# A two-layer transformer kernel: keys cut from 256 to 160 in its second attention, forgetting sums formed once, and the exponentials of a recurrence moved in the order of work

## The reference, cut to what matters

```
h  = x + rms(mixer(rms(x)))              # mixer: 8 heads "fox" + 8 heads "hgrn", w_in, w_out
h  = h + rms(conv_ffn(rms(h)))           # 3-tap convolution along the tokens, w_up, w_down
h  = h + rms((p @ w_proj) * sigmoid(rms(h) @ w_gate))
h  = h + neighbourhood_attention(rms(h)) # 16 heads, na_w_qkv, na_w_o
out= h + relu(rms(h) @ w1)**2 @ w2
```

## Time and profile before

| what | value |
|---|---|
| median of 3 runs | 2419.09 us |
| the profiled execution's own time | 2418.97 us |
| its span, first to last instruction | 2417.2 us |
| TensorE busy | 2405.5 us, 12352 records |
| VectorE busy | 1525.5 us |
| ScalarE busy | 1216.5 us |
| GpSimd busy | 110.4 us |
| TensorE's granted clock | 1.00 of full throughout |
| DMA | 451 MB, 57.6% of 16 engines by the weight queue |

### The profile page before, as it was taken

One profiled execution on the slowest core, in us unless ns is written; L12 is line 12 of the kernel. 1 busy time (PEld: TensorE's weight loads), 2 busy tenths in 40 slices (PEclk: granted clock), 3 DMA queues, 4 the chain that ended last, 5 costly groups with the idle time before them and its releaser, 6 DMA issues.

```text
span 2417.2 us, 30523 instructions
## 1 busy us (share of the span) xinstructions
PE 2405.5 (100%) x12352; PEld 2055.4 (85%) x12352; DVE 1525.5 (63%) x1788; ACT 1216.5 (50%) x1596; POOL 110.4 (5%) x122
## 2 busy tenths in 40 slices
PE   8999999999999999999999999999999999999999
PEld 7898988788888888888877888888888888888887
DVE  6676765577567657667666666665655555554654
ACT  6455444565445445445565655555443443443442
POOL 0221310000000000000000211000000000000000
PEclk9999999999999999999999999999999999999999
DMA  9566565556655655656655565455556556566664
GB/s 311 138 173 173 156 198 188 179 174 195 201 183 184 202 181 188 204 176 195 210 186 168 181 193 167 148 179 182 186 188 195 185 193 194 187 193 193 191 200 149
DMA packets 327132, 451.27 MB, mean 187 GB/s; under 512 B 14528, under 2 KB 209344, under 8 KB 326352
## 3 DMA queue, kind: packets, MB, share of 16 engines
q1 hardware_dynamic: 324592, 440.52, 57.6%
q0 software_dynamic: 2256, 8.80, 1.2%
q10 hardware_dynamic: 144, 0.01, 0.0%
HBM read 447.17 MB, written 2.10 MB: 186 GB/s over the span
## 4 chain that ended last, share of the span: by engine, by line
PE 97%; DVE 2%; issue 0%; ACT 0%; DMA 0%; POOL 0%; DVEq 0%; ACTq 0%
PE main L566 92%; PE aux L566 3%; DVE LO L1152 1%; DVE AR L1152 1%; PE aux L579 1%; PE aux L677 0%; PE aux L695 0%; ACT HI L810 0%; DVE AR L1329 0%; DVE XT L1155 0%; DMA COL<-in_cols 0%; DVE AR L1155 0%; PE aux L661 0%; DVE AR L1293 0%; DVE AR L1294 0%
## 5 line engine op out<-in xcount | busy, mean ns | idle before, releaser
L1152 DVE TENSOR_TENSOR LO<-RAW,HI 128x1024 fp32r<-128x1024 f32 (+2 forms) x833 | 1008.1, 1232 | 614.6 <-ACT HI L810 613.5
L810 ACT ACTIVATE HI<-RAW 128x1024 fp32r<-128x1024 f32 (+2 forms) x833 | 850.1, 1045 | 621.6 <-PE main L566 574.7
L566 PE MATMUL main<-XT,HI 128*128 128x512 f32 x2944 | 739.1, 393 | 0.0
L566 PE MATMUL main<-HI,YT 128*128 128x512 f32 x2240 | 693.6, 390 | 0.0
L566 PEld LDWEIGHTS main<-XT,HI 128*128 128x128 f32 x2944 | 529.8, 189 | 95.2
L566 PEld LDWEIGHTS main<-HI,YT 128*128 128x128 f32 x2240 | 420.5, 188 | 87.2
L566 PE MATMUL main<-HI,XT 128*128 128x512 f32 (+1 forms) x1472 | 458.1, 386 | 7.8 <-DVE LO L1152 7.7
L566 PE MATMUL main<-LO,YT 128*128 128x512 f32 x1120 | 435.8, 389 | 0.0
L566 PEld LDWEIGHTS main<-XT,LO 128*128 128x128 f32 x2944 | 401.6, 190 | 28.9
L566 PE MATMUL main<-XT,LO 128*128 128x256 f32 x2944 | 410.4, 282 | 0.0
L566 PEld LDWEIGHTS main<-HI,XT 128*128 128x128 f32 x1472 | 275.0, 188 | 60.0 <-DVE XT L1155 6.9
(11 more groups left out here) (87 smaller groups left out, 710.9 us busy)
## 6 DMA issues: line engine op xcount, KB each, us to landing
RAW<-in_mlp_w SPq DMA_DIRECT2D x256, 512.0 KB, 4.1
RAW<-in_w_up SPq DMA_DIRECT2D x176, 512.0 KB, 4.7
RAW<-in_na_w_qkv SPq DMA_DIRECT2D x96, 512.0 KB, 4.3
RAW<-in_w_in SPq DMA_DIRECT2D x95, 512.0 KB, 4.2
RAW<-in_w_down SPq DMA_DIRECT2D x88, 512.0 KB, 4.8
RAW<-in_w_out SPq DMA_DIRECT2D x32, 512.0 KB, 4.3
RAW<-in_w_ple_gate SPq DMA_DIRECT2D x32, 512.0 KB, 4.4
RAW<-in_na_w_o SPq DMA_DIRECT2D x32, 512.0 KB, 4.1
```

The source lines that it names most:

```text
L566: return L.e.matmul(out, l, r, start=start, stop=stop, skip_group_check=True)
L810: return L.e.activation(out, x, f, **kw)
L1152: return L.e.tensor_tensor(out, x, y, op)
```

## The change

1. **Token order.** From w_out's input on, the tokens lie by column of the grid and not by row (token = 4 x column + row). Where the natural order is needed or produced (fox and hgrn outputs, the FFN's input and its output, the residual's load, the final store), the reading or writing pattern is strided by 4 numbers (`by_column`, `by_row`). Neighbourhood attention itself needs no inner reordering any more.
2. **160 of 256 keys.** In that order, the keys that 128 queries need lie in one band of 160. Scores, bias, softmax and the copy after the transposes work on 2 x 160 numbers. The output product becomes three products of 160, 64 and 96 columns. The transposes keep their four, over a buffer whose borders are zeroed once.
3. **Forgetting sums once.** A step `f_sums` at slot 60 forms the sums of all 8 heads with two products, ScalarE writes them negated to CN (8 partitions), and for each head GpSimd's queue loads its row to 128 partitions (`f_row`), GpSimd adds the causal mask (`f_decay`), and VectorE adds the result to the logits in two instructions in place of one. `f_score` keeps two of its five products.
4. **Level exponentials.** The exponential leaves `h_decay` and becomes `h_exp`, one slot later, so it stands on ScalarE behind the next slot's rounding and no longer ahead of it.
5. **Second half of hgrn:** `h_out` and `h_rms` move from slots 105 and 107 to 108 and 110.

```diff
+        put(mid, j0 + 6, "h_exp", hf, 0)
         put(mid, j0 + 6, "h_weigh", hf, 0)
...
                 put(mid, at, "h_decay", hf, lvl)
+                put(mid, at + 1, "h_exp", hf, lvl)
                 put(mid, at + 1, "h_weigh", hf, lvl)
...
-        put(mid, j0 + 33, "h_out", hf)
-        put(mid, j0 + 35, "h_rms", hf)
+        put(mid, (j0 + 33, 108)[hf], "h_out", hf)
+        put(mid, (j0 + 35, 110)[hf], "h_rms", hf)
...
+    put(mid, 60, "f_sums")
-        for what, j in (("f_decay", j0 - 6), ("f_score", j0 + 2), ...
+        for what, j in (("f_row", j0 - 5), ("f_decay", j0 - 3), ("f_score", j0 + 2), ...
...
+        def by_column(ap):
+            return ap.rearrange("p (c r) -> p r c", r=4) ...
+        def by_row(ap, r=4):
+            return ap.rearrange("p (r c) -> p r c", r=r) ...
...
+            def f_sums():                                            # TensorE
+                mm(out[0:8, 0:256], LS[:, 0, :], tri, True, False)
+                mm(out[0:8, 128:256], LS[:, 1, :], tri[:, 0:128], False, True)
...
-                mm(out[:, 0:128], q[:, 0:128], k[:, 0:128], True, False)
-                mm(out[:, 0:128], B[:, 0, :], tri[:, 0:128], False, True)
-                mm(out[:, 128:384], q[:, 128:256], k, True, False)
-                mm(out[:, 128:384], B[:, 0, :], tri, False, False)
-                mm(out[:, 256:384], B[:, 1, :], tri[:, 0:128], False, True)
+                mm(out[:, 0:128], q[:, 0:128], k[:, 0:128], True, True)
+                mm(out[:, 128:384], q[:, 128:256], k, True, True)
...
-                mm(out[:, 0:256], q[:, 0:128], k, True, True)
-                mm(out[:, 256:512], q[:, 128:256], k, True, True)
+                mm(out[:, 0:160], q[:, 0:128], k[:, 96:256], True, True)
+                mm(out[:, 160:320], q[:, 128:256], k[:, 0:160], True, True)
...
-                mm(out[:, 0:256], VN[:, 0, ...], P[:, 0, :], True, False)
-                mm(out[:, 0:256], VN[:, 1, ...], P[:, 1, :], False, True)
+                mm(out[:, 96:256], v[0], P[:, 0:160], True, False)
+                mm(out[:, 96:160], v[1], P[:, 256:320], False, True)
+                mm(out[:, 0:96], v[1], P[:, 160:256], True, True)
...
+                    if ph == 1:                                      # ScalarE, FFN input; VectorE alike
+                        dst, src = by_row(dst), by_column(src)
...
+                if n < 22:                                           # ScalarE, FFN output; VectorE alike
+                    dst, src = by_column(dst), by_row(src)
...
+                out = banks[bank["f_score", h]]                      # VectorE
+                L.wait_ge(S("g_lb"), 2 * h + 2)
+                tt(P[:, 0:128], out[:, 0:128], CD[h % 2], ALU.add)
+                tt(P[:, 128:384], out[:, 128:384], CB[h % 2], ALU.add)
...
+            def f_row(h):                                            # GpSimd's queue
+                L.wait_ge(S("a_cn"), 1)
+                if h > 1:
+                    L.wait_ge(S("v_fl"), h - 1)
+                load(f"d_cb{h % 2}", CB[h % 2], <row h of CN, to 128 partitions>)
...
             def f_decay(h):                                          # GpSimd
+                L.wait_ge(S(f"d_cb{h % 2}"), 16 * (h // 2 + 1))
+                L.e.tensor_tensor(CD[h % 2], B[:, 0:128], causal, ALU.add)
+                L.e.tensor_tensor(B[:, 128:256], B[:, 128:256], causal, ALU.add)
```

More of the change, by code:

```diff
@@ L161, in stages @@
                 put(mid, at + 1, "h_far", hf)
-        put(mid, j0 + 33, "h_out", hf)
-        put(mid, j0 + 35, "h_rms", hf)
+        put(mid, (j0 + 33, 108)[hf], "h_out", hf)
+        put(mid, (j0 + 35, 110)[hf], "h_rms", hf)
         put(mid, (j0 + 35, 120)[hf], "h_gated", hf)
         put(mid, (j0 + 38, 122)[hf], "h_turn", hf)
+    put(mid, 60, "f_sums")
     for hp in range(4):
         j0 = 88 + 8 * hp
-        for what, j in (("f_decay", j0 - 6), ("f_score", j0 + 2), ("f_norm", j0 + 3), ("f_turn", j0 + 5), ("f_out", j0 + 7)):
+        for what, j in (("f_row", j0 - 5), ("f_decay", j0 - 3), ("f_score", j0 + 2), ("f_norm", j0 + 3), ("f_turn", j0 + 5), ("f_out", j0 + 7)):
             for h in (2 * hp, 2 * hp + 1):
@@ L273, in stage @@
                 take(("h_turn", rest[0], t), ("v_hyl", 2 * rest[0] + t + 1))
+        elif name == "f_sums":
+            take(("f_sums",), ("a_cn", 1))
         elif name == "f_score":
@@ L380, in program @@
         PF, PTF = [ar(16896, 384), ar(11776, 384)], [ar(17280, 384), ar(12160, 384)]
-        LB = [ar(19200, 2, 128), ar(12544, 2, 128)]
+        CB = [ar(19200, T), ar(12544, T)]
+        CD = [CST[:, C_CM + 128 + i * 128:C_CM + 256 + i * 128] for i in range(2)]
         MSKF = ar(8192, 8, 128)
@@ L527, in store @@
             def store(nb):
-                cs = slice(nb * 512, nb * 512 + 512)
-                L.wait_ge(S("v_h"), 56 + 2 * nb + 2)
-                L.e.dma_start(outv[:, :, cs], H[:, :, cs]).then_inc(S("d_out"), 16)
+                for t in range(2):
+                    L.wait_ge(S("v_h"), 56 + 2 * nb + t + 1)
+                    put(t, nb * 512, 512)
             def fetch_gate(nb):
@@ L727, in gate_value @@
                 x.then_inc(S("p_e"), 1)
-            work = {"e": gate_value, "turn": turn, "xq": turn_half, "h_score": h_score, "h_far": h_far, "h_out": h_out, "h_turn": h_turn, "f_score": f_score,
+            work = {"e": gate_value, "turn": turn, "xq": turn_half, "h_score": h_score, "h_far": h_far, "h_out": h_out, "h_turn": h_turn, "f_sums": f_sums, "f_score": f_score,
                     "f_turn": f_turn, "f_out": f_out, "n_turn": n_turn, "n_score": n_score, "n_prob": n_prob, "n_out": n_out,
@@ L1353, in h_turn @@
                     out = banks[bank["h_turn", hf, t]].rearrange("p (h t) -> p h t", h=4)
[L1354 to L1355 removed]
+                    c0 = 8 + 4 * hf
+                    hi, lo = [by_column(YT[:, c0:c0 + 4, i, :])[:, :, 2 * t:2 * t + 2, :] for i in range(2)]
+                    tt(lo, by_row(out, 2), hi.bitcast(F32), ALU.subtract).then_inc(S("v_hyl"), 1)
             def f_score(h):
@@ L1388, in n_turn @@
                 if i == 0:
-                    for r in range(2):
-                        rows = slice(r * 64, r * 64 + 64)
-                        x = L.e.tensor_scalar(dst[:, :, rows], src[:, :, rows][:, :, ::-1], gc, SCALE, ALU.mult, ALU.mult)
+                    x = L.e.tensor_scalar(dst, src[:, :, ::-1], gc, SCALE, ALU.mult, ALU.mult)
                 else:
@@ L1722, in bias0 @@
                     bias_rows(h)
-            work = {"h_abs": h_abs, "h_decay": h_decay, "h_weigh": h_weigh, "h_out": h_out, "f_decay": f_decay,
+            work = {"h_abs": h_abs, "h_decay": h_decay, "h_weigh": h_weigh, "h_out": h_out, "f_row": f_row, "f_decay": f_decay,
                     "n_prob": n_prob, "first_loads": first_loads, "more_loads": more_loads, "last_loads": last_loads,
@@ L1790, in constants @@
     c[:, C_TRI + 128:C_TRI + 256] = 1.0
-    col = 63 - i % 64
-    start = np.clip(col - 8, 0, 48)
-    k = np.arange(64)[None, :]
-    c[:, C_WIN:C_WIN + 64] = np.where((k >= start[:, None]) & (k < start[:, None] + 16), 0.0, NEG)
+    for t in range(2):
+        start = np.clip(63 - 32 * t - i // 4 - 8, 0, 48)
+        k = 24 - 24 * t + np.arange(40)[None, :]
+        c[:, C_WIN + 40 * t:C_WIN + 40 * t + 40] = np.where((k >= start[:, None]) & (k < start[:, None] + 16), 0.0, NEG)
     m = np.zeros((128, 8, 128), np.float32)
```

138 lines of the change are left out of this document (80 added, 58 removed).

## The result

The changed kernel takes 2403.23 us (median of 4 runs, 2402.82 to 2403.74), the kernel before 2419.19 us in the same session (4 runs, 2419.09 to 2419.53). The ratio is 0.9934, 95% interval 0.9917 to 0.9951: 16.0 us less. Predicted were 2403.0 us and 2400 to 2410.5. The profiled execution took 2403.74 us, its span is 2402.0; before 2418.97 and 2417.2.

A forecast was written before the change was run, and what follows sets the result against it. TensorE was taken as the bound. From 2418.97 us, 14.1 of products (7.0 + 5.2 + 2.6 - 0.7) and 2.1 of stops came off and 0.3 for strided passes was added: 2403.1, forecast 2403 us, range 2400 to 2410.5.

The forecast's parts named there:

- What bounds the kernel: Whole kernel: TensorE alone sets the time while ScalarE waits for HI; product time taken out comes off the end.
- Fox: Fox's `f_score`, five products to two: 3.07 us for two heads falls to 1.31, saving 7.0 us for eight heads.
- Scores: Neighbourhood scores, 256 to 160 columns: 3.45 us for four heads falls to 2.16, saving 5.2 us for four groups.
- Outputs: Neighbourhood output, two products to three: 1.73 us for two heads falls to 1.40, saving 2.6 us for sixteen.
- The sums: `f_sums` at slot 60: two added products and a switch to an aside and back add 0.7 us (0.5 to 0.9).
- Exponentials: hgrn's 344-column stage: exponentials behind the rounding remove 2.1 us of TensorE stops; hgrn's second half has none to give back.
- The second rival: Fox's slots: VectorE becomes the bound, 60 of 70 us, and fox's 7.0 us are lost: 2410 us; chance 0.07.
- Strided passes: ScalarE and VectorE passes with a step of 4 numbers: 0.3 us added at the FFN's input; cover at its output.
- The first rival: FFN's input: strided passes cost more than plain ones where TensorE waits for them, +3.7, 2407 us; chance 0.12.
- The third rival: FFN's output: strided passes, from factor 4, outrun 4.0 us of cover; at factor 6, 2460 us; chance 0.03.
- The cover of the DMA and of GpSimd: Fox's forgetting rows: loads come seven slots (20 us) earlier, GpSimd has 48 of 75 us free; nothing booked.
- the unnamed losses: Anywhere in the kernel: losses not named in the prediction that eat most of the gain; chance 0.05.

The follow-up runs named there:

- run 3: Only the forgetting sums formed once and loaded, on the kernel before, with exponentials and `h_out` at their old slots: 2416.38 us, ratio 0.9988.
- run 1: The changed kernel with each level exponential put back at the slot of its decay, ahead of the next rounding: 2407.99 us, ratio 0.9953.
- run 7: The changed kernel with ScalarE's strided pass at the FFN's output made four times instead of once: 2463.82 us, ratio 1.0185.
- run 9: The changed kernel with ScalarE's strided pass at the FFN's output made twice instead of once: 2408.06 us, ratio 0.9954.
- run 6: The changed kernel with the FFN's output written in natural order, without strided writes, leaving out the reordering of tokens: 2403.28 us, ratio 0.9934.
- run 10: The changed kernel with GpSimd's `f_decay` right behind the load of its row, so GpSimd waits for the DMA: 2403.81 us, ratio 0.9935.
- run 11: The changed kernel with final stores going to 128 consecutive rows, leaving out the order of the output's rows: 2402.78 us, ratio 0.9932.
- run 2: The kernel before with nothing but the level exponentials moved one slot later: 2416.67 us, ratio 0.9989.

## Why the prediction was right

**What bounds the kernel** was right: TensorE, and every product taken out came off the end.

**Sizes of the products.** Fox: 7.0 forecast, 7.15 measured from mark to mark. Scores: 4 x 1.29 = 5.2 forecast, 4 x (3.45 - 2.17) = 5.1. Outputs: 2.6 forecast, 8 x (1.73 - 1.41) = 2.6. The 0.135 us for 160 columns, a value between two rows, came out as 0.136. Reading pieces of the chain instead of the records' own durations is what made this work: the records overlap, the pieces don't.

**The sums** were mis-sized a little: `f_sums` took 0.75 us in its piece and 0.19 around it, 0.94 for 0.7, just outside the 0.5 to 0.9 given for it. That its products have a side of only 8 columns did not make them cheaper.

**Exponentials** in the 344-column stage: 2.1 forecast, 2.4 measured; 59.0 us forecast for the stage, 58.7 measured, and no wait for LO. But the sentence that the second half of hgrn "has no stops to give back" missed what the edit does there. It has none in the kernel before; it has 3.4 us of them (7.15 - 3.78, run 3) as soon as fox's products alone are gone. The moved exponentials keep 1.9 of these away (run 1). The other 1.5 are kept away by something else in the change, by the chain of run 3 the later `h_out`, which the prediction booked at nothing. I treated the edits as a sum, and they are not one. That fox's 7.0 us came in whole rests on edits that were priced at nothing there, so this part of the hit is partly luck.

**The second rival** (VectorE the bound in fox's slots) had 0.07. It is half true of run 3, where 3.4 of fox's 7 us are lost, and not true of the change. The share of busy time said nothing here: 58.2 of 75 us with stops, 63.2 of 75 without. I had compared shares (60 of 70) where the closed turn of two engines counts.

**Strided passes.** I took 0.3 us at the FFN's input; it was nothing there. The first rival had the size of the effect right (1.7 times) and the place wrong: reads of PSUM with the step are free (1.57 and 1.66 us, unchanged), passes that write to SBUF with it take 1.11 and 1.12 us for 0.63 and 0.69, at the FFN's output, where there is cover. By the Trainium skill ("SBUF — State Buffer", Door 1: The DMA port swizzle) an access in SBUF pays as soon as each number is in a new line of 16 bytes. The trace agrees for ScalarE's writes, and for VectorE's write and read together. What it says of PSUM's smaller lines it says of matmuls; no run here bears on that, and for ScalarE's and VectorE's reads of PSUM the step cost nothing.

**The third rival's cover** was wrong in kind, though its case did not arise. I measured the spare time at one place, 4.0 us at the last chunk of a short group, and let it serve each pair. Runs 7 and 9 show that what counts is the length of a turn, 21.47 to 21.49 us in the changed kernel against TensorE's 22.35, so 0.9 us to spare. With plain passes the turn is 20.82 us (run 6) and the spare time 1.5 us, and 1.32 (k - 1) passes it from about k = 2.2 on, not from 4. The strided passes used some 0.65 of these 1.5 us; the forecast was nearer to this edge than I said.

**The cover of the DMA and of GpSimd** held: 7 slots were forecast as enough, and with GpSimd longer in wait (run 10) the time moved by no more than its spread.

**Not forecast:** 0.35 us of the last store, costed at nothing since it "keeps its size"; its rows lie apart (run 11). And 0.8 us at the start, of which most differs from run to run; the median of the runs, 2403.23, holds some of it perhaps. The near hit of the total, 0.2 us, owes something to luck: 15.9 us were forecast, and in the profiled execution the edits gave 16.4 where they work, less 1.2 for start and tail. The chances hold a small slip too: without the third rival and the unnamed losses they add up to 0.92, not 0.91.

## What to carry to other kernels

Where two engines work in turn, compare the length of their turn with that of the engine they feed, and not shares of busy time: an added pass is free up to the difference and is paid in every turn from there on. Such a turn can be read where the engine that it feeds doesn't hold it up, as in the first two pairs of the FFN. Edits that shorten such a turn and edits that shorten the engine it feeds must be costed together: the moved exponentials bring 2.5 us on the kernel before (run 2) and 4.8 on the changed one (run 1). Price products by pieces of the chain of waits at several widths, and look for the floor: below 128 columns of this type a further cut saves nothing and adds records, as the version with two products of 160 shows (2400.48 us).

## What the runs showed of the hardware

- ScalarE writing 4-byte numbers to SBUF with a step of 16 bytes takes 1.11 us for 128x512 instead of 0.63; VectorE writing and reading SBUF with it takes 1.12 instead of 0.69; reading PSUM with the same step (128x256) costs neither anything (1.57 and 1.66 us for four, as before). A VectorE pass in runs of two out of four numbers cost nothing more either, 0.68 us.
- A record of TensorE for fp32 costs 0.108 to 0.11 us up to 128 columns and 0.00084 us per column above (0.136, 0.163 and 0.216 at 160, 192 and 256).
- A last store of 128 KB whose neighbouring partitions go to rows 64 apart lands 0.3 to 0.35 us later than one in consecutive rows (3.6 to 3.7 against 3.3 us from VectorE's last instruction to the end).
- In run 7, behind a stop of 2.34 us of TensorE, the granted clock was 0.80 on the mean from 605 to 607 us, 0.57 from 607 to 610 and 1.00 from 610 to 615. The chain of waits has no piece of TensorE there, so it costs nothing.
